# Choosing PSUM banks inside the list scheduler, loading the first conditioning weights by whole rows, holding back later quarters of x, and tracking small vectors by 8 bytes

## The chip, the cores and the metric

The kernel runs on the 8 cores of one Trainium2 chip. Each core computes one element of the batch, with no exchange between the cores; all of them read the same weights from HBM. The time of a run is the device time of the slowest core, in microseconds (us).

## What is computed

Two layers, each a mixing sub-layer and a channel sub-layer, over x of 2048 tokens by 1024 features. Float32 in and out; the kernel holds x as float32 and feeds TensorE with bf16.

```
mod = silu(c) @ w_ada + b_ada;  sh1, sc1, gt1, sh2, sc2, gt2 = split(mod, 6)
h = rms_norm(x, g_mix) * (1 + sc1) + sh1
q_a, k_a, v_a, q_b, k_b, v_b, gate_a, gate_b = split(h @ w_in)
q, k = rope(rms_norm(per head))                      # both mixers
y_a = banded attention (window 128, 8 heads, sinks) @ w_o_swa
y_b = block-sparse attention (own block + top 3 past blocks of 256) @ w_o_moba
x = x + gt1 * ((sigmoid(gate_a) * y_a + sigmoid(gate_b) * y_b) @ w_out)
h = rms_norm(x, g_mlp) * (1 + sc2) + sh2
x = x + gt2 * (square(relu(h @ w_up)) @ w_down)
```

## The kernel before

A Python program records every instruction of both layers with its operands (`Sched.add`), puts them in order with a list scheduler (`Sched.schedule`), and then emits one queue for each engine with semaphore waits (`emit`). Each engine works off its queue strictly in that order. Dependencies come from keys: an operand covers keys of 256 bytes in SBUF and of one 2048-byte bank in PSUM, and for each key the last writer and the readers are known. `window` gives each recorded operation a due time `vt`; among the operations that could start on an engine, the scheduler takes the one with the lowest `vt`. Its own costs of instructions and DMAs (L550 to L604) only decide the order.

The work of a layer, in the order in which it is recorded, over four quarters s of 512 tokens, each in a 16 KB slot of SBUF (`xslot`):

- **kv_stage(s)**: `norm_in_place` (squares on ScalarE at L776 or GpSimd at L779, a sum over features by 8 matmuls into one bank, Ln and Exp, then 8 pairs of scalar_tensor_tensor on VectorE, L577, and Identity at L791 that write h over half of the slot), then five `qk_item` (8 matmuls, Square, one matmul, Ln, Exp, a product, one matmul, three rotary products, using three banks) and four `v_block` (two banks each): 24 bank uses in a stage.
- **q_stage(s)**: eight `qk_item`. Those of quarters 2 and 3 run beside attention and use banks 6 and 7 only.
- **att_stage(s)** on banks 0 to 5, beside **c_mix** and **c_out** of the quarter before on banks 6 and 7; c_mix(3), c_out(2) and c_out(3) follow on all eight.
- **norm(s)** for the channel sub-layer, then `mlp_up` and `mlp_down` in four groups g over the four quarters, all eight banks.

A bank is chosen when the operation is recorded: `bank()` (L612) hands out the allowed banks in rotation. So a tile waits for all users of the tile that had its bank eight `bank()` calls earlier in the recorded order, whatever the scheduler makes of the order.

At the start SP issues the loads of x (`load_x`, 16 of 512 KB; 16 float32 128x128 transposes through PSUM for each two), the position rows and the spill of each x slot to HBM; GpSimd issues the weights. `ada_group(l, g, buffer)` loads 256 columns of w_ada (8 runs of 1 KB for each partition, written as 512 B of bf16) and makes two columns of `mod` from 16 one-column matmuls. Of layer 0, groups 0 to 7 (shift and scale of the mixing norm) come first, through five buffers; groups 8 to 23 are recorded behind the kv stages, four to each, and are first used by c_out and `norm`. `mod`, the gains and `A1` of a layer lie in one 256-byte stretch, and each group writes into it while each norm and each qk_item reads it. `rope_table` makes four tables, kept in HBM (`cs_d`), in two SBUF buffers `csb`. `load_w1` loads the five parts of w_in for q, k and v.

`norm` and `norm_in_place` share one buffer `nrm_r` and two `nrm_t` at T0, which is also where attention's probabilities and the operand `mixs[1]` of c_out(3) lie.

## Time and profile before

| | us |
|---|---|
| median of 3 runs | 2548.09 (2540.18 to 2724.18) |
| the profiled execution, device time | 2552.81 |
| its span on the slowest core (core 3) | 2551.3 |
| TensorE busy in it | 2179.7 (85%) |
| VectorE, ScalarE, GpSimd busy | 1138.2, 1126.0, 162.6 |
| spans of the eight cores | 2527.4 to 2551.3 |

Busy times are of the profiler's own modelled ends for matmuls, so a busy TensorE is not TensorE at its peak; the granted clock says at which of its levels (1.2 or 2.4 GHz) it ran. "Idle before, released by" on a row is the time in which the engine did nothing just before, and what ended it. Layer 0 runs from 0 to about 1343 us, layer 1 from there to the end.

### The profile page before, as it was taken

To read this page: it belongs to the slowest core of one execution; us is meant where nothing else is said; L and a number is where in the kernel's file an instruction comes from. 1 tells how busy PE (TensorE), PEld (TensorE's weight loads), DVE (VectorE), ACT (ScalarE), POOL (GpSimd) and SP (SyncE) were. 2 spreads that over 40 slices of the span, in tenths; PEclk is the share of its full clock that TensorE was granted. 3 is DMA by queue.
4 is the path that set the end of the run, shared out by engine and by line. 5 is a ranking of instruction groups with operands and counts; after the bars stand their busy time and mean duration, and the time that the engine had idled before them with its cause. 6 is when DMAs were issued, how large, how long until landed. Compare 5 with 4: busy or idle time off the path is not lost.

```text
span 2551.3 us, 33260 instructions; the slowest of 8 cores (2527.4 to 2551.3 us)
## 1 busy us (share of the span) xinstructions
PE 2179.7 (85%) x11604; PEld 905.6 (35%) x11604; DVE 1138.2 (45%) x1991; ACT 1126.0 (44%) x1650; POOL 162.6 (6%) x167
## 2 busy tenths in 40 slices
PE   1346687889899999999996687889899989999996
PEld 1323232323233444444442332232323434444443
DVE  1255576533322464444445677542422364444432
ACT  1444467666665341111115567857575452111122
POOL 1010120000000001010000020000000100000000
PEclk7677789999999999999997889999999999999998
DMA  9973420600002937373511020240000560331011
GB/s 212 195 134 42 63 46 7 94 34 1 34 1 50 156 51 95 41 106 42 100 67 58 17 50 9 37 64 34 1 34 1 107 92 14 53 51 16 1 67 66
DMA packets 122497, 149.28 MB, mean 59 GB/s; under 512 B 3808, under 2 KB 110560, under 8 KB 119264
## 3 DMA queue, kind: packets, MB, share of 16 engines
q0 software_dynamic: 108368, 85.14, 25.1%
q1 hardware_dynamic: 13968, 62.02, 7.1%
q8 instruction: 98, 1.61, 0.3%
q14 instruction: 63, 0.52, 0.1%
HBM read 205.02 MB, written 27.26 MB: 91 GB/s over the span
## 4 chain that ended last, share of the span: by engine, by line
PE 76%; ACT 8%; issue 5%; DVE 5%; DMA 4%; another core or an unknown queue 1%; POOL 0%; SPq 0%; ACTq 0%; DVEq 0%; POOLq 0%
PE PS L520 76%; ACT SB L546 4%; DMA SB<-w_ada 4%; DVE SB L577 2%; DVE SB L551 2%; ACT SB L791 1%; ACT SB L758 1%; PE PS L528 1%; ACT L546 1%; DMA SB<-w_in 1%; ACT SB L585 1%; DVE SB L567 0%; DVE SB L591 0%; ACT SB L776 0%
## 5 line engine op out<-in xcount | busy, mean ns | idle before, releaser
L520 PE MATMUL PS<-SB 128*128 128x512 bf16 (+7 forms) x11332 | 2138.9, 362 | 333.0 <-ACT SB L791 91.7
L520 PEld LDWEIGHTS PS<-SB 128*128 128x128 bf16 (+2 forms) x11332 | 866.3, 100 | 1598.9 <-issue 827.0
L546 ACT ACTIVATE SB<-PS 128x512 f32<-128x512 f32 (+4 forms) x902 | 642.8, 732 | 1032.6 <-PE PS L520 1010.2
L577 DVE SCALAR_TENSOR_TENSOR SB<-PS,SB 128x512 bf16<-128x512 f32 (+1 forms) x680 | 492.2, 728 | 669.4 <-ACT SB L546 348.6
L551 DVE TENSOR_TENSOR SB<-SB 128x512 bf16<-128x512 f32 (+5 forms) x452 | 254.6, 575 | 170.5 <-ACT SB L546 151.2
L551 DVE TENSOR_TENSOR SB<-PS,SB 128x512 f32<-128x512 f32 (+2 forms) x248 | 143.6, 585 | 172.5 <-PE PS L520 115.4
L577 DVE SCALAR_TENSOR_TENSOR SB<-SB,PS 128x512 f32<-128x512 f32 x128 | 87.6, 687 | 224.0 <-PE PS L520 148.0
L546 ACT ACTIVATE SB<-SB 128x512 f32<-128x512 f32 x226 | 139.9, 626 | 19.0 <-DVE SB L551 9.9
L577 DVE SCALAR_TENSOR_TENSOR SB<-SB 128x512 f32<-128x512 f32 x148 | 103.8, 726 | 38.6 <-ACT SB L546 25.9
L546 ACT ACT_TABLE_LOAD x67 | 86.0, 1283 | 40.1 <-DVE SB L551 21.2
L546 ACT ACTIVATE SB<-PS,SB 128x512 f32<-128x512 f32 x120 | 82.4, 687 | 47.4 <-PE PS L520 46.8
L585 ACT COPY SB<-PS 128x512 f32<-128x512 f32 x59 | 34.0, 586 | 141.6 <-PE PS L528 126.9
L604 POOL DMA_DIRECT2D SB<-w_ada x48 | 42.4, 885 | 449.6 <-PE PS L520 446.5
L791 ACT ACTIVATE SB<-SB 128x512 bf16<-128x512 f32 x64 | 45.0, 721 | 48.9 <-DVE SB L577 35.3
L528 PE MATMUL PS<-SB 128*128 128x128 f32 (+1 forms) x272 | 47.2, 327 | 20.9 <-DMA SB<-x 15.7
L746 POOL TENSOR_TENSOR SB<-SB 128x512 bf16<-128x512 f32 x20 | 20.8, 1038 | 622.4 <-PE PS L520 622.4
L528 PEld LDWEIGHTS PS<-SB 128*128 128x128 f32 (+1 forms) x272 | 39.6, 170 | 29.0 <-issue 24.9
L758 ACT ACTIVATE SB<-SB 128x512 bf16<-128x512 f32 x62 | 42.9, 719 | 13.1 <-DVE SB L577 13.0
L743 ACT ACTIVATE SB<-SB 128x512 bf16<-128x512 f32 x44 | 27.6, 627 | 43.8 <-DVE SB L577 43.7
L551 POOL TENSOR_TENSOR SB<-SB 128x512 bf16<-128x512 f32 (+1 forms) x26 | 37.2, 1431 | 134.5 <-DVE SB L551 90.7
L776 ACT ACTIVATE SB<-SB 128x512 bf16<-128x512 f32 x58 | 34.7, 624 | 15.4 <-PE PS L520 13.1
L587 DVE CAST SB<-PS 128x128 bf16<-128x128 f32 (+1 forms) x17 | 8.2, 480 | 59.8 <-PE PS L520 59.8
(22 smaller groups left out, 162.8 us busy)
## 6 DMA issues: line engine op xcount, KB each, us to landing
SB<-w_ada POOLq DMA_DIRECT2D x48, 512.0 KB, 8.4
SB<-w_in POOLq DMA_DIRECT2D x16, 1024.0 KB, 14.6
xsp<-SB SPq DMA_DIRECT2D x8, 2048.0 KB, 9.9
SB<-xsp SPq DMA_DIRECT2D x16, 1024.0 KB, 7.3
SB<-w_up POOLq DMA_DIRECT2D x16, 1024.0 KB, 13.0
SB<-w_down POOLq DMA_DIRECT2D x16, 1024.0 KB, 20.2
SB<-x SPq DMA_DIRECT2D x16, 512.0 KB, 15.7
SB<-cs SPq DMA_DIRECT2D x16, 512.0 KB, 4.4
```

Of the source, the lines that this page charges most:

```text
L520: ins = e.matmul(o, l_, rr, start=a, stop=b)
L528: S.add([('pe', lambda e, o=out.ap, i=in_.ap, d=ident.ap: e.transpose(o, i, d), 0.235 if in_.dt == F32 else 0.1)], list(in_.keys) + list(i ...
L546: S.add([('act', lambda e, o=out.ap, i=in_.ap: e.activation(out=o, in_=i, func=func, **kw), d)], r, out.keys, tab=TABS.get(func))
L551: return e.tensor_tensor(out=o, in0=a, in1=b, op=op)
L577: S.add([('dve', lambda e, o=out.ap, x=in0.ap, y=in1.ap: e.scalar_tensor_tensor(out=o, in0=x, scalar=a, in1=y, op0=op0, op1=op1), cost('dv ...
L585: alts.append((g, lambda e, o=out.ap, i=in_.ap: e.copy(out=o, in_=i), cost(g, n)))
L604: S.add([(eng, lambda e, o=out.ap, i=in_.ap: e.dma_start(out=o, in_=i), 0.45 if eng == 'sp' else 1.0)], in_.keys, out.keys, dma_key=key, n ...
L743: return e.activation(out=o, in_=i, func=AF.Square)
L746: return e.tensor_tensor(out=o, in0=i, in1=i, op=ALU.mult)
L758: return e.activation(out=o, in_=i, func=AF.Identity, bias=b)
L776: return e.activation(out=o, in_=i, func=AF.Square)
L791: return e.activation(out=o, in_=i, func=AF.Identity, bias=b)
```

## The change

It has five parts.

1. **Banks.** `bank()` goes away. A PSUM tile (`Tile`) is recorded without a bank and gets one in `schedule`, at the moment when its first operation is put in order: of the allowed banks the one that is free first by the scheduler's account (`place`). Tiles of one `line` get banks in their recorded order, and a tile with `more=True` gets one only if at least two of its allowed banks have no tile with operations still to be put in order. Allowed banks stay as they were.
2. **Tracking.** Operands between TR and TR+6144 (constants, `mod`, gains, routing vectors) have keys of 8 bytes instead of 256.
3. **First conditioning weights.** Groups 0 to 7 of layer 0 become eight loads of 128 rows by 2048 columns into eight buffers, 128 one-column matmuls that add up row block by row block in one bank, and one addition.
4. **x held back.** Quarter 1 of x is issued only when the sixth of these loads has landed, quarter 2 after the keys' weights (kb), quarter 3 after the values' (vb). Tables 2 and 3 of `rope_table` get buffers of their own in the last x slot, so 0 and 1 stay in `csb` and are not loaded again in the first two kv stages.
5. **Norm buffers.** `norm_in_place` rotates three `nrm_r` and four square buffers (one and two before). `norm` gets a scale row and one temporary of its own, apart from attention's buffers, and its 8 sum matmuls are recorded behind all 8 squares.

The scheduler also accounts for two DMA queues that share the bandwidth instead of one.

```diff
+        def place(tile):
+            if tile.line is not None and tile.line[tile.line[0]] is not tile:
+                return None, 1e9
+            if tile.more and sum(bank_free[b] < 1e8 for p in tile.allow for b in p) < 2:
+                return None, 1e9
+            best = None
+            for p in tile.allow:
+                f = max(bank_free[b] for b in p)
+                if best is None or f < best[1]:
+                    best = (p, f)
+            return best
...
+            for tl in op['tiles']:
+                if tl.banks is None:
+                    tl.banks = place(tl)[0]
+                    if tl.line is not None:
+                        tl.line[0] += 1
+                    for b in tl.banks:
+                        op['deps'].update(bank_users[b])
...
         def sb(off, shape, dt):
-            return SBA.view(off, shape, dt)
+            return (SBV if TR <= off < TR + 6144 else SBA).view(off, shape, dt)
...
-        nrm_r = sb(T0, (512,), F32)
+        nm_r, nm_t = sb(T0 + 30464, (512,), F32), sb(T0 + 32512, (512,), F32)
+        nrm_rs = [sb(T0 + o, (512,), F32) for o in (0, 8192, 10240)]
...
-        for g in range(8):
-            ada_group(0, g, (adab + adab2)[g % 5])
+        first = [sb(RW + 32768 + i * 4096, (2048,), BF16) for i in range(6)] + [
+            sb(T0 + 12288, (2048,), BF16), sb(T0 + 18176, (2048,), BF16)]
+        for k in range(8):
+            dma(first[k], Raw(w_ada_d[0, k * 128:(k + 1) * 128, 0:2048]), 'pool')
+        pm0 = ps((16,))
+        for k in range(8):
+            for j in range(16):
+                mm(pm0[:, j:j + 1], first[k][:, j * 128:(j + 1) * 128], silc[:, k:k + 1], k == 0 and j == 0, k == 7 and j == 15)
+        tt(modv(0)[:, 0:16], pm0, sb(VB + 16 * 4, (16,), F32), ALU.add)
         ada_fin(0, 0)
         W1 = load_w1(0, -70.0)
+        gates = [first[5].keys, W1['kb'].keys, W1['vb'].keys]
         for t in range(4, NT):
             at(-60.0 + t)
-            load_x(t)
+            load_x(t, gates[t // 4 - 1])
...
         def qk_item(wcols, s, gain, dest, cs):
-            pin = ps(bank(), (512,))
+            pin = ps((512,), more=True, line='qk')
```

GpSimd's queue at the start of the program. Before: five conditioning loads (128x8x256), then four of w_in, then the rest of the conditioning loads.

```order
L604 DMA SB<-cb 128x768
L604 DMA SB<-w_ada 128x8x256 x5
L604 DMA SB<-w_in 128x8x256
L604 DMA SB<-w_in 128x8x512 x3
L604 DMA SB<-w_ada 128x8x256 x6
L604 DMA SB<-w_in 128x8x512
```

Now:

```order
L696 DMA SB<-cb 128x768
L696 DMA SB<-w_ada 128x2048 x8
L696 DMA SB<-w_in 128x8x256
L696 DMA SB<-w_in 128x8x512 x3
L696 DMA SB<-w_ada 128x8x256 x3
L696 DMA SB<-w_in 128x8x512
L878 TENSOR_TENSOR SB<-SB 128x512 x2
```

All of the first conditioning weights now stand ahead of w_in; before, three of eight stood behind four loads of w_in.

ScalarE's queue where layer 0 passes from one kv stage to the next (before, from stage 1 to 2). L776 are the squares of the next quarter's norm, L791 its Identities that write h; L546 with SB<-PS,SB is an Ln, with SB<-SB an Exp, and L585 copies values out of PSUM.

```order
L546 ACTIVATE SB<-PS 128x512
L776 ACTIVATE SB<-SB 128x512 x2
L546 ACTIVATE SB<-PS,SB 128x512
L776 ACTIVATE SB<-SB 128x512
L546 ACTIVATE SB<-SB 128x512
L776 ACTIVATE SB<-SB 128x512 x3
L546 ACTIVATE SB<-PS,SB 128x512
L776 ACTIVATE SB<-SB 128x512
L546 ACTIVATE SB<-SB 128x512
L791 ACTIVATE SB<-SB 128x512 x8
L546 ACTIVATE SB<-PS 128x512
```

Now, inside a kv stage of layer 0 (L890 is the Identity, L638 the activations of the qk items, L677 the copies of values):

```order
L890 ACTIVATE SB<-SB 128x512
L638 ACTIVATE SB<-PS 128x512
L677 CAST SB<-PS 128x128
L890 ACTIVATE SB<-SB 128x512
L638 ACTIVATE SB<-PS,SB 128x512
L677 CAST SB<-PS 128x512
L638 ACTIVATE SB<-SB 128x512
L890 ACTIVATE SB<-SB 128x512
L638 ACTIVATE SB<-PS 128x512
L677 CAST SB<-PS 128x128
L890 ACTIVATE SB<-SB 128x512
```

The eight Identities no longer stand in one block between the last item of a stage and the first of the next; they are spread between the items and the value copies of the stage before.

## Rows read from the trace of the kernel before

**Rows 1.** The page: span, busy times, the span in 40 slices.
```profile
PE 2179.7 (85%) x11604; PEld 905.6 (35%) x11604; DVE 1138.2 (45%) x1991; ACT 1126.0 (44%) x1650; POOL 162.6 (6%) x167
PE   1346687889899999999996687889899989999996
PEclk7677789999999999999997889999999999999998
```

**Rows 2.** Busy time by stretch: stretch, its us, then each engine's busy us, clock, DMA, GB/s.
```profile
0.00:130.00 130.00, 34.44 (x264) 28.29 (x264) 28.79 (x61) 37.46 (x59) 14.05 (x20) 0.66 1.04 203
130.00:305.00 175.00, 102.89 (x669) 49.34 (x670) 92.28 (x186) 80.16 (x135) 16.07 (x17) 0.77 0.49 77
305.00:880.00 575.00, 512.84 (x2800) 179.05 (x2797) 256.89 (x490) 347.13 (x469) 43.45 (x41) 0.97 0.25 45
1343.00:1496.00 153.00, 98.60 (x483) 44.65 (x482) 90.20 (x168) 87.15 (x148) 3.11 (x3) 0.79 0.09 31
880.00:1343.00 463.00, 458.26 (x2460) 211.22 (x2459) 209.97 (x319) 105.45 (x173) 32.58 (x36) 1.00 0.48 74
```

**Rows 3.** Timeline of the start: start us, us, engine, line, what, idle before and releaser.
```profile
2.29 4.41 POOL L604 DMA_DIRECT2D SB<-w_ada  x5
6.64 3.56 POOL L604 DMA_DIRECT2D SB<-w_in  x4
28.35 0.88 POOL L604 DMA_DIRECT2D SB<-w_ada  x1 [18.15 <-PE PS L520]
97.64 0.56 PE L520 MATMUL PS<-SB 128*128 128x1 bf16 x16 [27.49 <-DMA SB<-w_ada]
106.65 0.17 DVE L577 SCALAR_TENSOR_TENSOR SB<-SB 128x8 f32<-128x8 f32 x1
```

**Rows 4.** DMA queues from 30 to 64 us: packets, MB, share of 16 engines' time.
```profile
q0 software_dynamic: 4848, 2.75, 67.7%
q1 hardware_dynamic: 866, 4.63, 42.7%
```

**Rows 5.** The page's DMA queues, whole span: packets, MB, share of 16 engines.
```profile
q0 software_dynamic: 108368, 85.14, 25.1%
```

**Rows 6.** Waits of TensorE, 130 to 350 us: total us, times, longest.
```profile
PE PS L520 <- ACT SB L791: 43.9, 4, 11.5
PE PS L520 <- DMA SB<-w_ada: 20.7, 4, 8.0
PE PS L520 <- DVE SB L551: 13.9, 2, 7.4
```

**Rows 7.** Waits of TensorE, 1280 to 1500 us.
```profile
PE PS L520 <- ACT SB L791: 47.7, 4, 13.0
```

**Rows 8.** Timeline of GpSimd: loads of c weights, released by the last kv matmuls.
```profile
305.59 0.88 POOL L604 DMA_DIRECT2D SB<-w_in  x1 [28.93 <-PE PS L520]
1496.09 0.94 POOL L604 DMA_DIRECT2D SB<-w_in  x1 [35.36 <-PE PS L520]
```

**Rows 9.** Timeline of TensorE where layer 1 begins.
```profile
1324.67 19.16 PE L520 MATMUL PS<-SB 128*128 128x512 bf16 x88
...
1357.35 21.68 PE L520 MATMUL PS<-SB 128*128 128x512 bf16 x114 [9.48 <-ACT SB L791]
```

**Rows 10.** Timeline of TensorE where layer 0's channel sub-layer begins.
```profile
879.15 17.64 PE L520 MATMUL PS<-SB 128*128 128x512 bf16 x81 [1.77 <-DVE SB L577]
```

**Rows 11.** Groups of instructions by shape: busy us, mean ns, idle before.
```profile
L528 PE MATMUL PS<-SB 128*128 128x128 f32 x256 | 43.7, 333 | 19.1 <-DMA SB<-x 15.7 <-ACT SB L585 1.7 <-DVE SB L551 1.5
L577 DVE SCALAR_TENSOR_TENSOR SB<-SB 128x512 f32<-128x512 f32 x144 | 103.2, 742 | 38.1 <-ACT SB L546 25.9 <-ACT SB L791 4.2 <-ACT SB L758 3.9
L791 ACT ACTIVATE SB<-SB 128x512 bf16<-128x512 f32 x64 | 45.0, 721 | 48.9 <-DVE SB L577 35.3 <-DVE SB L567 13.6
L551 DVE TENSOR_TENSOR SB<-SB 128x512 bf16<-128x512 f32 x153 | 107.1, 700 | 10.9 <-DVE SB L551 0.5 <-DVE SB L577 0.5 <-DVE SB L568 0.4
```

**Rows 12.** The page's DMA issues: count, KB each, median us from issue to landing.
```profile
SB<-w_ada POOLq DMA_DIRECT2D x48, 512.0 KB, 8.4
```

224 lines of the change are left out of this document (143 added, 81 removed).

## Prediction, made before the changed kernel ran

> **What bounds the kernel now.** I read the page first, for the share of TensorE by slice, then the busy times by stretch, then TensorE's waits in the stretches where it is not busy, and last the timeline at the places where those waits end. TensorE is busy 2179.7 of 2551.3 us and the two other large engines 44 to 45% each, so TensorE bounds the whole; but the 40 slices show that it does so unevenly: digits of 1 to 6 in the first five slices, a dip to 6 and 6 where layer 1 begins, 8 and 9 elsewhere [rows 1]. By stretch [rows 2]: 0 to 130 us TensorE is busy 34.4 of 130 with the DMA engines full (share 1.04); 130 to 305 (the four kv stages of layer 0) 102.9 of 175 at a granted clock of 0.77; the same stages of layer 1, 1343 to 1496, 98.6 of 153 at 0.79; attention and the c stages, 305 to 880, 512.8 of 575; the channel sub-layer 458.3 of 463. The last two have little to give. What can move lies in the first 305 us and in the 153 of layer 1.
>
> The first 106.7 us are a wait for conditioning weights. Five of the eight loads are issued at 2.3 us, then four loads of w_in; the sixth is issued at 28.4 us, when a buffer comes free, and its matmuls run at 97.6, after 27.5 us of idle TensorE. A1, which every h needs, is there at 106.65 [rows 3]. The kv stages end at about 305.6 and 1496.1, when the last matmul that reads their weights lets GpSimd load the next ones [rows 8]. Inside them TensorE waits 43.9 and 47.7 us, four times each, for the Identities of the in-place norm [rows 6, 7]: the norm of the next quarter does not overlap the matmuls of this one.
>
> **Part by part: the start.** At present the DMA engines are full, so this is a sum of engine time. From 30 to 64 us queue 0 moves 4848 packets, 2.75 MB, in 67.7% of 34 us of 16 engines: 76 ns for a packet of 0.57 KB. Queue 1, with x, takes 42.7% for 866 packets of 5.3 KB: 268 ns [rows 4]. The first eight groups are 8192 packets of 512 B, 39 us of all 16 engines. Now they are 1024 packets that read 8 KB and write 4 KB. No such packet is in the trace. Bounds: by the 5.3 KB packet, 268 ns, it is 17 us; by reading 8 KB at that packet's 20 GB/s, 400 ns, it is 26 us; at the small packets' rate per byte it stays 39. I take 25, since the float32 side is what has to be read. Ahead of A1 there are then also x's first quarter (2 MB, 6.5 us at 20 GB/s on 16 engines), a spill of 2 MB (6.5) and 4 to 5 for position rows and tables. With a start at 2.3 us: 45 us for A1 instead of 106.7.
>
> The Trainium skill (DMA: Bandwidth & Descriptors, Specifications) puts line rate at transfers of 512 B and more, which would leave nothing to gain from whole rows, since the old packets have that size on the writing side. The rows of queue 0 do not bear it out, at 7.5 GB/s written for one engine against 17 to 20 for the large packets of queue 1. By the rule A1 would stand at 59 us if the old 39 us are kept, 14 later.
>
> Then h(0) costs 8 pairs of 742 and 721 ns [rows 11] on two engines that overlap, 7 us: 52. The weights follow at the mean packet of queue 0, 0.251 x 2551 x 16 / 108368 = 94.5 ns [rows 5], 1024 packets and 6 us for each of kva, kb, vb. With x's quarter 1, held until the sixth load has landed, and a part of 2 between them, vb lands at about 25 + 18 + 31 (queue 1 so far: two and a half quarters of x, a spill, positions, tables) + 2 = 76 us. So stage 0 is fed through, about half of it after 76.
>
> **The kv stages of layer 0.** Matmul columns that TensorE has to do in 130 to 305: 102.9 us at clock 0.77. A stage holds 90 matmuls of 512 columns and 32 narrow ones; at the end of the channel sub-layer, at full clock, 88 matmuls of 512 take 19.16 us [rows 9], 0.218 each, so 19.6, about 2 for the narrow ones and 2 for its conditioning groups: 23.5 us, 94 for four. To that come 192 float32 transposes of quarters 1 to 3, which now fall behind 50 us instead of before 118; at 333 ns, mostly at the low clock [rows 11], 64, and at half of that 32; I take 36, the clock being mostly high. VectorE has 92.3 us in this stretch and ScalarE 80.2 [rows 2], plus 12 copies each, of about the length of a product: both near or under 100, so TensorE is longest with 130. Because banks are taken when work is put in order, and not eight calls back in the recorded order, and because the norm has its own rotating buffers, the squares and Identities of quarter s+1 stand between the items of quarter s (the two pieces of ScalarE's queue). Finer keys take away the order between each conditioning group's addition and each norm and gain, which stand behind the 20.7 and 13.9 us of waits for w_ada and L551 [rows 6]. I expect most of 43.9 + 20.7 + 13.9 = 78.5 us to go, and 20 to 25 to stay or come back: clock lows (130 us at 0.92 instead of 1.0 is 11) and waits for w_ada, which TensorE still takes in the order of its queue. 52 + 130 + 11 + 13 = 206, against 305.6: **minus 100**. The 16 groups behind need 16 x 1024 x 76 ns / 16 = 78 us of DMA between about 90 and 200, beside spills of 6 MB (20 us): it fits, with little to spare.
>
> **The kv stages of layer 1.** The norm of quarter 0 now takes place under the last mlp_down; before, it stood open from 1343.8 to 1357.4 [rows 9]. Its squares still cannot start before the last mlp_up has read the buffers they share. Four stages hold 4 x 21.5 = 86 us of TensorE at full clock; VectorE's 90.2 [rows 2] lose some 10 to GpSimd, which takes more of the 700 ns products [rows 11] (57 of them in its new queue, 26 in the old, half of the difference in each layer). Three engines near 80 to 90 us each, now overlapped: at 80% packing 110. In the new queue one norm, the last, still has its eight Identities in one block (7 us); that is within the 110. 153 - 110 = **minus 43**.
>
> **The rest.** The channel norm no longer waits for attention's buffers and c_out(3); TensorE idles there 1.8 us [rows 10], and I allow 1.2 for the gaps behind it: minus 3 for each layer, **minus 6**. Its single temporary makes a norm 8 x 1.7 = 13.6 us long, under 28 us of mlp matmuls for each quarter: nothing; without that cover 7 us once for each layer. Attention has the same order of exponentials and items in both queues (the sixteen last q items stand behind 0 to 59 exponentials in both), and the same banks: 0, with 10 either way. Two cs loads fewer: hidden.
>
> Sum: 2552.8 - 100 - 43 - 6 = 2404. The profiled execution lies 5 above the median; I say **2405** for the median, the 4 not being worth a digit.
>
> **The rivals.**
> - *Conditioning loads take over as the bound.* Each group's 16 matmuls stand at a fixed place in TensorE's queue, the three buffers are refilled only behind them, and GpSimd's squares and products stand behind waiting loads. From issue to landing one takes 8.4 us [rows 12], of which 78 / 16 = 5 are engine time; if the rest costs TensorE 2 us for each of the 16 groups, that is 32 us; the kv stages end near 238. For it: 20.7 us of such waits today at a slower pace. Against it: three are in flight at a time. 2437.
> - *The packing is better.* If the clock stays at 1.0 in both layers' stages and the waits go to nothing, 24 us go in layer 0 and 15 in layer 1: 2365. Against it: the clock was 0.77 and 0.79 with 59 to 64% busy.
> - *The norm chain stays on the path.* If ScalarE's and GpSimd's in-order queues only move the wait from Identities to something else (positions, rotary tables in front of GpSimd's squares, spills before h may be written), the kv stages keep 46 us each and only the start is won: 2552.8 - 60 - 6 = 2487. Against it: the order.
> - *Slower: starving on two banks.* With banks 6 and 7 alone, `more` wants both without open tiles, so a new item's or gate's 8 matmuls may be put in order only when the product that reads the last bank is. There are 64 such tiles in a layer (16 items, 48 gates). If each adds one reader, 0.75 us and the way there and back, 1.7 us, and attention's matmuls do not fill it, it is 64 x 2 x 1.7 = 218 us: 2620. It decides from 1.2 us a tile on. Against it: TensorE is 89% busy there with attention's own matmuls [rows 2], and its neighbours in the queue are as before.
>
> **Chances.** Forecast 0.60 (its own range 2380 to 2425), conditioning loads 0.16, better packing 0.12, norm chain 0.08, starving 0.04. A measurement of this kernel can tell about 2% from no change, so 2497 is the border. The first three are faster; of the norm chain, at 2487, six in ten; so 0.93 faster, 0.05 within 2%, 0.02 slower. The range takes in better packing and conditioning loads with 25 us more: 2360 to 2460.
>
> **What would show it.** A1's addition in the timeline at 40 to 60 us, all eight loads landed before any of w_in; the loads of c weights behind the kv stages issued near 205 instead of 305.6, and 110 us instead of 153 behind the end of layer 0's channel sub-layer; TensorE's waits for the Identity line under 15 us in each layer; a clock of 0.85 or more in both stretches; 575 us from the end of the kv stages to the channel sub-layer, as now. Wrong would be: A1 later than 70 (packets of 8 KB no better than small ones), waits of TensorE for w_ada above 30 us, VectorE or ScalarE over 90% busy in the kv stages, or more than 590 us for attention.

## The result, and the profile after

The changed kernel takes 2435.26 us (median of 4 runs, 2432.23 to 2547.38) against 2544.14 for the kernel before beside it (2539.87 to 2724.18). The ratio is 0.957, with a 95% interval of 0.954 to 0.960: faster by 109 us. The forecast was 2405 (a sum of 149 us less, counted from the profiled execution of the kernel before). The time lies inside the range on record and 30 us above the forecast. In the longest executions of both kernels the cores of one die ran at a lower granted clock; ratios and profiles leave such executions out.

The page of the profile after, core 6 (busy time and share; then busy tenths in 40 slices, the granted clock in tenths of full speed, and the DMA engines' busy tenths):

```profile
span 2430.7 us, 32875 instructions; the slowest of 8 cores (2414.1 to 2430.7 us)
PE 2144.9 (88%) x11383; PEld 903.5 (37%) x11604; DVE 1128.1 (46%) x1950; ACT 1105.1 (45%) x1631; POOL 235.1 (10%) x222
...
PE   1469878897999999999998777889899999999997
...
PEclk9879889999999999999999898999999999999998
DMA  9966405100105837474320201600010542240012
```

Against [rows 1] the start has shrunk: TensorE is at 7 to 9 from the fourth slice on (before, from the sixth), and the dip where layer 1 begins has gone from 6 to 7. The page lacks 221 of TensorE's matmul records (11383 against 11604 weight loads), and its busy time with them. The six cores that have all records show 2166.5 to 2171.0 us, against 2172.5 to 2179.7 on the six such cores of the kernel before. So the work is nearly the same, some 7 us less, and almost the whole gain is idle time.

Busy times by stretch, the same five stretches as [rows 2], at this kernel's own borders (kv stages of layer 0 end at 232, the first w_up load is at 760, layer 0 ends at 1269, the kv stages of layer 1 at 1383):

```profile
core 6: us, PE busy (x) PEld busy (x) DVE busy (x) ACT busy (x) POOL busy (x), PEclk, DMA share, GB/s
0.00:130.00 130.00, 44.77 (x321) 30.20 (x326) 40.88 (x78) 43.35 (x67) 14.20 (x23) 0.90 1.00 210
130.00:232.00 102.00, 82.28 (x561) 41.98 (x572) 76.11 (x151) 63.76 (x117) 36.30 (x31) 0.90 0.55 94
232.00:760.00 528.00, 461.12 (x2552) 157.86 (x2599) 237.40 (x463) 339.26 (x457) 47.29 (x43) 0.95 0.21 38
1269.00:1383.00 114.00, 88.73 (x468) 41.38 (x478) 87.00 (x156) 74.04 (x132) 37.27 (x27) 0.90 0.11 41
760.00:1269.00 509.00, 505.63 (x2643) 234.80 (x2696) 226.68 (x341) 115.87 (x189) 38.68 (x45) 1.00 0.53 83
```

In the kv stages TensorE is now busy 78 to 81% of the time (some records of this core are missing, so slightly more) at a clock of 0.90, where it was 59 to 64% at 0.77 and 0.79 [rows 2].

A marker in each trace cuts the span into six parts: GpSimd's first load of c weights (the end of the kv stages, the answer to [rows 8]), its first w_up load, and SP's last spill of the layer.

```profile
232.08 0.87 POOL L696 DMA_DIRECT2D SB<-w_in  x1
759.94 0.89 POOL L696 DMA_DIRECT2D SB<-w_up  x1 [12.88 <-PE PS L612]
1268.86 0.32 SPq L696 DMA_DIRECT2D xsp<-SB  x1
1383.02 0.96 POOL L696 DMA_DIRECT2D SB<-w_in  x1 [30.29 <-PE PS L612]
1901.21 0.96 POOL L696 DMA_DIRECT2D SB<-w_up  x1 [19.96 <-PE PS L612]
```

| us | start and kv stages, layer 0 | attention | channel | kv stages, layer 1 | attention | channel | span |
|---|---|---|---|---|---|---|---|
| before | 305.6 | 520.6 | 518.1 | 151.8 | 509.1 | 546.1 | 2551.3 |
| after | 232.1 | 527.9 | 508.9 | 114.2 | 518.2 | 529.5 | 2430.7 |
| difference | -73.5 | +7.3 | -9.2 | -37.6 | +9.1 | -16.6 | -120.6 |
| on record | -100 | 0 | -3 | -43 | 0 | -3 | -149 |

TensorE's waits in layer 0 from 130 to 233 us, and in layer 1 from 1260 to 1384 (releaser: us in total, times, longest), which answer [rows 6] and [rows 7]:

```profile
PE PS L612 <- ACT SB L890: 12.2, 2, 9.4
PE PS L612 <- ACT SB L875: 2.0, 4, 0.6
PE PS L612 <- DVE SB L669: 1.8, 4, 0.9
...
PE PS L612 <- ACT SB L890: 13.6, 1, 13.6
PE PS L612 <- ACT SB L875: 7.1, 6, 4.9
PE PS L612 <- DVE SB L669: 2.6, 3, 1.1
```

L890 is the Identity of the in-place norm. TensorE waited for it 43.9 and 47.7 us, four times a layer. In layer 0 the norm of quarter 0 now falls before 130 us, so the whole stretch from 0 to 233 us has to be counted; there it is

```profile
PE PS L612 <- ACT SB L890: 16.0, 3, 9.4
```

that is 3.7 us for the norm of quarter 0, 9.4 for quarter 1, nothing for quarter 2 and 2.8 for quarter 3. In layer 1 the one wait stands before the last quarter: three stages run through and the fourth waits for its whole norm.

```profile
1363.73 20.57 PE L612 MATMUL PS<-SB 128*128 128x512 bf16 x110 [13.57 <-ACT SB L890]
```

### The profile page after: what moved, and what is told of

It is laid out like the page before. It is cut to its first block, busy times and chain, and to the rows that moved or that the text cites. A ratio compares the mean times of both kernels' runs of the same rounds, so it can differ in the third digit from the quotient of the medians.

```text
span 2430.7 us, 32875 instructions; the slowest of 8 cores (2414.1 to 2430.7 us)
## 1 busy us (share of the span) xinstructions
PE 2144.9 (88%) x11383; PEld 903.5 (37%) x11604; DVE 1128.1 (46%) x1950; ACT 1105.1 (45%) x1631; POOL 235.1 (10%) x222
## 4 chain that ended last, share of the span: by engine, by line
PE 81%; ACT 6%; issue 5%; DVE 5%; DMA 2%; another core or an unknown queue 0%; POOL 0%; SPq 0%; ACTq 0%; DVEq 0%; POOLq 0%
PE PS L612 79%; ACT SB L638 4%; DVE SB L643 2%; DMA SB<-pos 2%; DVE SB L669 2%; PE PS L620 1%; ACT L638 1%; ACT SB L677 0%; ACT SB L890 0%; DVE SB L659 0%; POOL SB L893 0%; DVE SB L683 0%; DMA out<-SB 0%; SPq L696 0%
## 5 line engine op out<-in xcount | busy, mean ns | idle before, releaser
L612 PE MATMUL PS<-SB 128*128 128x512 bf16 (+6 forms) x11111 | 2115.1, 362 | 231.0 <-ACT SB L638 78.8
L612 PEld LDWEIGHTS PS<-SB 128*128 128x128 bf16 (+2 forms) x11332 | 864.9, 100 | 1454.9 <-issue 679.6
L638 ACT ACTIVATE SB<-PS 128x512 f32<-128x512 f32 (+4 forms) x902 | 641.6, 732 | 973.2 <-PE PS L612 953.7
L669 DVE SCALAR_TENSOR_TENSOR SB<-PS,SB 128x512 bf16<-128x512 f32 (+1 forms) x680 | 493.9, 727 | 665.8 <-ACT SB L638 343.1
L643 DVE TENSOR_TENSOR SB<-SB 128x512 bf16<-128x512 f32 (+5 forms) x421 | 234.0, 567 | 146.3 <-ACT SB L638 132.5
L643 DVE TENSOR_TENSOR SB<-PS,SB 128x512 f32<-128x512 f32 (+3 forms) x241 | 141.7, 596 | 132.7 <-ACT SB L638 75.3
L669 DVE SCALAR_TENSOR_TENSOR SB<-SB,PS 128x512 f32<-128x512 f32 x128 | 87.5, 686 | 214.0 <-PE PS L612 138.4
L638 ACT ACTIVATE SB<-SB 128x512 f32<-128x512 f32 (+1 forms) x226 | 139.6, 624 | 27.3 <-DVE SB L659 11.6
L669 DVE SCALAR_TENSOR_TENSOR SB<-SB 128x512 f32<-128x512 f32 (+1 forms) x148 | 118.4, 810 | 32.5 <-ACT SB L638 16.1
L643 POOL TENSOR_TENSOR SB<-SB 128x512 bf16<-128x512 f32 (+1 forms) x57 | 76.9, 1356 | 348.0 <-DVE SB L669 299.8
L638 ACT ACTIVATE SB<-PS,SB 128x512 f32<-128x512 f32 x120 | 81.8, 685 | 36.5 <-PE PS L612 34.7
L620 PE MATMUL PS<-SB 128*128 128x128 f32 (+1 forms) x272 | 56.6, 314 | 37.6 <-DMA SB<-x 28.6
L677 ACT COPY SB<-PS 128x512 f32<-128x512 f32 x59 | 34.0, 583 | 117.7 <-PE PS L620 90.1
L620 PEld LDWEIGHTS PS<-SB 128*128 128x128 f32 (+1 forms) x272 | 39.3, 162 | 55.0 <-issue 43.0
L858 ACT ACTIVATE SB<-SB 128x512 bf16<-128x512 f32 x60 | 43.2, 720 | 23.6 <-DVE SB L669 22.7
L890 ACT ACTIVATE SB<-SB 128x512 bf16<-128x512 f32 x51 | 36.3, 720 | 26.4 <-DVE SB L669 23.9
L696 POOL DMA_DIRECT2D SB<-w_up x16 | 14.1, 881 | 281.5 <-PE PS L612 281.5
L875 ACT ACTIVATE SB<-SB 128x512 bf16<-128x512 f32 x47 | 27.2, 621 | 27.8 <-PE PS L612 26.8
L842 ACT ACTIVATE SB<-SB 128x512 bf16<-128x512 f32 x46 | 28.8, 627 | 21.8 <-DVE SB L669 21.8
```

The costliest lines, as they stand in the source:

```text
L612: ins = e.matmul(o.ap, l_.ap, rr.ap, start=a, stop=b)
L620: S.add([('pe', lambda e, o=out, i=in_, d=ident: e.transpose(o.ap, i.ap, d.ap), 0.235 if in_.dt == F32 else 0.1)], list(in_.keys) + list(i ...
L638: S.add([('act', lambda e, o=out, i=in_: e.activation(out=o.ap, in_=i.ap, func=func, **kw), d)], r, out.keys, tab=TABS.get(func))
L643: return e.tensor_tensor(out=o.ap, in0=a.ap, in1=b.ap, op=op)
L669: S.add([('dve', lambda e, o=out, x=in0, y=in1: e.scalar_tensor_tensor(out=o.ap, in0=x.ap, scalar=a, in1=y.ap, op0=op0, op1=op1), cost('dv ...
L677: alts.append((g, lambda e, o=out, i=in_: e.copy(out=o.ap, in_=i.ap), cost(g, n)))
```

## Experiments: which part does it

Each kernel below is the changed kernel with the edit shown, or where it is said the kernel with split keys; its spans are cut by the same markers, on its slowest core unless others are named. Intervals of a ratio are 95%. A time without a ratio is that of the profiled execution.

**Banks taken in rotation again**, in the recorded order of each bank; the rules `line` and `more` go with it, all else is kept:

```diff
+            if tile.fix is not None:
+                for b in tile.fix:
+                    if tile.bankq[b][tile.bankq[b][0]] is not tile:
+                        return None, 1e9
+                return tile.fix, max(bank_free[b] for b in tile.fix)
...
+            if allow is None:
+                t.fix = nxt('bank', pool_banks[0])
```

> The changed kernel with one part undone: PSUM banks are again handed out in rotation when a tile is recorded (tiles of one bank strictly in recorded order, no rule of two free banks). Keys of 8 bytes, whole-row conditioning loads, held x and the norm buffers stay. Theory A, the choice of banks while ordering is what lets the in-place norm run under the stage before: the holes of about 9 us before each stage come back in both layers, the kv stages take about 145 us in layer 1 instead of 115, and the time is 2495 to 2515 us. Theory B, the norm's own rotating buffers and the finer keys are enough: under 2450 us and still about 115 us in layer 1.

Measured: ratio 1.011 (1.009 to 1.014), 2563.95 us, in the theory's direction and further than it said. The kv stages of layer 0 end at 283.6 and those of layer 1 last 149.3; the channel sub-layers take 528.4 and 557.6 us. TensorE's waits in the kv stages of layer 1:

```profile
PE PS L636 <- ACT SB L914: 50.1, 4, 13.7
```

L914 is the Identity here: four waits of 12 us, as before [rows 7]. Without the choice of banks the four other parts together leave the kernel slower than it was, so that choice carries the layer 1 gain, most of layer 0's (51.5 of 73.5 us), and it is what makes the rest fit. The choice of banks with the four other parts undone was not run, so what it is worth alone is not shown.

**Only the start** (whole-row weights, x held back and the tables' own buffers; rotation, 256-byte keys and the old norm buffers):

> Only the start is changed: whole-row conditioning loads into eight buffers, x held back, tables 2 and 3 in buffers of their own. Banks in rotation, keys of 256 bytes, one scale row and two square buffers for the in-place norm, the channel norm sharing attention's buffers. Theory A, the start is worth what A1 gained, 38 us (106.7 to 68.5), and the rest of the 109 comes from the kv stages: 2495 to 2510 us, with 150 us again in layer 1's stages. Theory B, the start carries most, since DMA-bound work moves with it: under 2465 us.

Measured: ratio 0.995 (0.993 to 0.997), 2526.75 us, above both ranges. The kv stages of layer 0 end at 290.1, 15.5 us earlier than before, and those of layer 1 last 151.0. A1 is there at 65.4 us and not at 106.7 [rows 3], and yet only 15 of these 41 us reach the end of the kv stages. The start alone is worth about 0.5%. This kernel is faster than the rotation kernel, which has the finer keys and the new norm buffers besides: under rotation these two cost more than they bring.

**x not held back**:

```diff
-            load_x(t, gates[t // 4 - 1])
+            load_x(t)
```

> The changed kernel with quarters 1 to 3 of x no longer held back, all else kept. Theory A, x's large packets crowd out the weights: A1 moves from 68.5 to 80 us or later, and the time is 2445 to 2460 us. Theory B, the DMA engines are full to 160 us with the same bytes whatever the order, and A1 waits for the rotary tables, not for the loads: 2428 to 2442 us, the values' weights landing within 5 us of 97 and the kv stages of layer 0 ending within 6 us of 232.

Measured: 2444.5 us in the profiled execution, 12 more than with the hold; kv stages end at 251.8. The time borders on theory A's, but A1 does not come later: it is there at 64.5 us, 4 earlier than with the hold. TensorE's waits from 0 to 252 us:

```profile
PE PS L612 <- DMA SB<-w_ada: 41.1, 2, 30.0
PE PS L612 <- ACT SB L890: 35.9, 3, 15.0
```

The hold is worth 20 us in the kv stages of layer 0, of which 12 are taken back in the attention stretch behind them (515.6 instead of 527.9): without it the transfers of x push a conditioning load from its place and TensorE stands 30.0 us before it.

**Keys of 256 bytes everywhere**:

```diff
-        SBV = Arena('SBV', sbt, 8)
+        SBV = Arena('SBV', sbt, 256)
```

> The changed kernel with keys of 256 bytes for the small vectors again, all else kept. Theory A, the additions of the conditioning groups and the norms and gains are put in a fixed order again, and a norm waits for four loads of w_ada: layer 0's kv stages 15 to 30 us longer, layer 1 unchanged, 2450 to 2465 us. Theory B, the norms wait for the same loads anyway through the engines' queues and the full DMA engines: 2430 to 2440 us.

Measured: ratio 0.959 (0.957 to 0.962), the same as the changed kernel within the intervals, but not by the same road. The kv stages of layer 0 end at 266.8, 35 us later, with waits for w_ada back (17.4 us in four); and the two attention stretches take 513.3 and 500.1 us, 14.6 and 18.1 less. So the finer keys win 35 us in one place and lose 33 in two others, and the prediction, which counted only the first, had taken attention as unchanged. The time fell into theory B's range, whose ground (the norms wait for the same loads anyway) did not hold; theory A had the ground and half of the size.

## Experiments: where the finer keys lose

The keys cover two sets of vectors: constants, `mod`, gains and `A1`; and, behind them, what routing uses (block means, their padded form, gate scores, ranks, biases). One run for each:

```diff
-            return (SBV if TR <= off < TR + 6144 else SBA).view(off, shape, dt)
+            return (SBV if TR <= off < TR + 4608 else SBA).view(off, shape, dt)
```

The second run has `TR + 4608 <= off < TR + 6144` instead. In both, three small views are taken through `sb` too, so that readers and writers have the same keys.

> Keys of 8 bytes only for the constants, mod, gains and A1; the routing vectors (block means, their padded form, gate scores, biases, ranks) get keys of 256 bytes again. Theory: the 35 us that fine keys win in the kv stages of layer 0 come from mod and A1, and the 15 and 18 us that they cost in the two attention stretches come from the routing vectors. Then the kv stages end near 232, the stretch from there to the first w_up load takes 513 us in layer 0 and 500 in layer 1, and the time is 2400 to 2405 us. Rival: the 15 and 18 us are no property of either set of keys but of which order the scheduler happens to find: 518 to 530 us in one layer or both, 2420 to 2440 us.

> The complement: keys of 8 bytes only for the routing vectors, 256 bytes for the constants, mod, gains and A1. Theory: kv stages of layer 0 end near 267 us as with 256 bytes everywhere, attention stretches of 528 and 518 us as in the changed kernel, 2465 us. Rival (order found by chance): the kv stages near 267, attention anywhere between 500 and 530, 2433 to 2465 us.

Measured with 8 bytes for the first set only: 2394.1 us in the profiled execution, 2403.4 in a second one. The kv stages end at 230.4, attention takes 504.2 and 504.2, and layer 1's kv stages 114.7. With 8 bytes for routing only: ratio 0.963 (0.960 to 0.966), kv stages at 266.6, attention 509.1 and 520.5. The win belongs to the first set in both runs. The loss follows the second set in layer 1 (518 and 521 with fine routing keys, 500 and 504 without) and less cleanly in layer 0 (528 and 509 with, 513 and 504 without): there part of it is the order that the scheduler happens on. Among all kernels that choose banks while ordering, the two attention stretches sum to 1008 to 1016 us in the five with split keys and 1013 in the one with 256 bytes everywhere, and to 1030 to 1046 in the five with fine routing keys. In layer 1 no core of the first six takes more than 507.5 us and none of the others less than 512.7; in layer 0 the two sets of cores overlap. (With rotation it is 1043 with fine keys, 1018 in the kernel with only the start changed and 1030 in the kernel before.) TensorE's waits in the attention stretch of layer 0, in the changed kernel and then with split keys:

```profile
PE PS L612 <- ACT SB L638: 38.3, 38, 2.8
PE PS L612 <- DVE SB L643: 21.4, 27, 2.1
PE PS L612 <- issue: 4.5, 22, 0.5
```

```profile
PE PS L612 <- ACT SB L638: 27.6, 38, 2.6
PE PS L612 <- DVE SB L643: 18.8, 29, 1.8
```

The same waits: these two lines went from 59.7 to 46.4 us. Which instruction of the routing is ordered worse with fine keys was not isolated. Taking them back wins 38 us of the span in the profiled executions (2392.5 against 2430.7), and 1.5 percentage points in the ratios of the two kernels below that add an edit to the split keys (0.942 against 0.957).

## Experiments: what holds the start

The last addition before A1 stands at 68.2 us, not at 45. The rows of VectorE ahead of it in the changed kernel, with that addition, then those of ScalarE and of TensorE, where L875 are the squares of the first norm and L659/L669 the arithmetic of the rotary tables:

```profile
56.18 0.43 DVE L679 CAST SB<-SB 128x512 f32<-128x512 int32 x1 [6.80 <-DMA SB<-pos]
...
68.24 0.17 DVE L643 TENSOR_TENSOR SB<-PS,SB 128x16 f32<-128x16 f32 x1 [1.89 <-PE PS L612]
```

```profile
58.74 0.63 ACT L638 ACTIVATE SB<-SB 128x512 f32<-128x512 f32 x1 [11.64 <-DVE SB L659]
60.07 0.63 ACT L638 ACTIVATE SB<-SB 128x512 f32<-128x512 f32 x1 [0.70 <-DVE SB L669]
60.60 1.13 ACT L875 ACTIVATE SB<-SB 128x512 bf16<-128x512 f32 x2
```

```profile
61.88 1.44 PE L612 MATMUL PS<-SB 128*128 128x512 bf16 x3 [16.11 <-ACT SB L875]
```

The eight loads had all landed by 45 us (the last of their packets starts at 42.9). The last 16 conditioning matmuls stand in TensorE's queue behind the norm's sum, that behind squares in ScalarE's queue, those behind the Sin of table 2, and that behind a position row whose load was issued only when the row before had been used. Two kernels move A1 in opposite directions. First, position rows in four buffers:

```diff
-            posi, x = sb(P0, (512,), I32), sb(P0 + 2048, (512,), F32)
+            posi, x = sb(RW + 16384 + s * 2048, (512,), I32), sb(P0 + 2048, (512,), F32)
```

> The four position rows get four buffers, so that their loads are issued together instead of one behind each table; nothing else changes. Theory: in the changed kernel A1's addition at 68 us was held by the rotary tables (ScalarE's Sin of table 2 at 59, the squares of the first norm behind it, the last 16 conditioning matmuls behind the norm's sum), not by its weights, which had landed by 45. Then A1 comes at 48 to 54, and quarter 1 of x is issued near 45 instead of 61. How much of these 15 us reaches the end: theory says 10, the kv stages of layer 0 end near 222, 2425 us. Rival: the DMA engines are full until 160 us in either case, so A1 comes early but the values' weights still land near 97 and the kv stages end at 229 to 234: 2433 to 2437 us.

Measured: ratio 0.951 (0.947 to 0.955), 2426.4 us in the profiled execution. The addition is at 64.6 instead of 68.2, the kv stages end at 232.8, the attention of layer 0 takes 514.9. The theory's 48 to 54 was wrong; the rival's end was right, and the time is below the rival's because attention is shorter. Second, the first weights by columns again, into the eight buffers:

```diff
-        for k in range(8):
-            dma(first[k], Raw(w_ada_d[0, k * 128:(k + 1) * 128, 0:2048]), 'pool')
...
+        for g in range(8):
+            ada_group(0, g, sb(first[g].off, (8, 256), BF16))
```

> One part undone: layer 0's first conditioning weights come again as eight loads of 256 columns (8192 packets that write 512 bytes), but into the eight separate buffers, all ahead of w_in; everything else as in the changed kernel. Theory (the price on record: small packets cost 76 ns of an engine each, 39 us of all 16; whole rows showed 268 to 337 ns for 1024 packets, about 19): the eighth load lands near 65 us instead of 45, and because the DMA engines stay full until about 160 us everything behind it is 20 us later as well: the values' weights at 115 instead of 97, the kv stages of layer 0 end near 248 instead of 232, 2450 us. Rival (a written 512 bytes is already at full rate): the eighth load again near 45 and 2435 us.

Measured: ratio 0.953 (0.950 to 0.957), not slower. The last addition is at 76.6, 8 us later, and the kv stages end at 229.8, 2 us earlier. Queue 0 (packets, MB, share of 16 engines) in the column kernel from 0 to 62 us, then in the changed kernel from 0 to 45; both have moved the same 4.56 MB by then:

```profile
q0 software_dynamic: 8653, 4.56, 64.8%
```

```profile
q0 software_dynamic: 1632, 4.56, 66.4%
```

0.648 x 62 is 40 us of all engines, 0.664 x 45 is 30: whole rows save 10 us, not the 20 that this run was built to show. The expectation had divided a window's time by all its packets, of which a part are small. By size, the 1024 packets that write 4096 bytes took 409 ns each in the changed kernel (26 us of all engines), and those that write 512 bytes 72 ns in the column kernel (37 us for 8192). So about 10 us of DMA time and 8 us of A1 are really saved, and none of it reaches the end.

> Split keys (2394 us) together with the four position rows in buffers of their own. Alone, the position rows brought A1 from 68 to 65 us, not to 50, the end of the kv stages stayed at 232.8, and the attention stretch of layer 0 was 13 us shorter (515 instead of 528). Theory: that gain was of the same kind as the split keys' (another order found for the routing), so it doesn't add: 2390 to 2397 us. Rival: the two are independent and add: 2382 us.

Measured: ratio 0.942 (0.940 to 0.945), 2402.2 us in the profiled execution, 5 above the theory's range: with split keys the position rows add nothing, as the theory said; their gain alone was in attention.

## Experiments: why the kv stages end at 230 to 233

In the changed kernel and in six edits of it (column loads, position rows, split keys, the last two together, and the two that follow, which stand on the split keys) the kv stages of layer 0 ended between 229.8 and 233.1 on the slowest core, wherever A1 stood. TensorE's rows between 109 and 131 us show what stands there (12 groups of four float32 transposes of x between 108.6 and 133 us, of which some are shown):

```profile
110.01 0.63 PE L620 MATMUL PS<-SB 128*128 128x128 f32 x4 [0.61 <-ACT SB L677]
...
114.57 1.09 PE L620 MATMUL PS<-SB 128*128 128x128 f32 x4 [0.93 <-ACT SB L677]
116.48 1.08 PE L620 MATMUL PS<-SB 128*128 128x128 f32 x4 [0.82 <-ACT SB L677]
```

Each group waits for ScalarE's copy of the one before, as it must if all of them go through one bank. (No row names the bank; with two banks kept for them, below, the order one by one is gone.) Two attempts took away what was suspected first. **Two banks kept for the transposes:**

```diff
+        XB = [(b,) for b in range(6, 8)]
...
-                pv = ps((4, 128))
+                pv = ps((4, 128), allow=XB if t >= 4 else None)
...
+                pool_banks[0] = [(b,) for b in range(6)] if l == 0 and s < 2 else ALL
                 kv_stage(l, s, W1)
```

> On top of the kernel with split keys (8 bytes for constants and mod, 256 for the routing vectors; 2394 us): the transposes of x's quarters 1 to 3 may use PSUM banks 6 and 7 only, and the items of the first two kv stages banks 0 to 5 only. In the changed kernel 12 groups of four transposes from 108 to 131 us follow one another through a single bank, each behind ScalarE's copy of the one before (1.5 to 2.0 us a group, TensorE idle 0.6 to 0.9 before each), since open tiles hold the others. Theory: this stands on the path to norm(1) and stage 1; with two banks a group costs its own 1.1 us, the row of groups ends about 10 us earlier, and so do the kv stages: end near 222 instead of 230, 2384 us. Rival: the DMA and the clock set the end of the kv stages, as two earlier runs hint, where an A1 of 65 or 77 us instead of 68 left the end at 230 to 233: again 229 to 233, 2392 us. Second rival: six banks are too few for the items: 240, 2402 us.

Measured: 2402.6 us in the profiled execution, kv stages end at 232.8. The transposes no longer go one by one, and in their place TensorE stands at a conditioning group:

```profile
125.17 2.72 PE L612 MATMUL PS<-SB 128*128 128x1 bf16 x21 [18.31 <-DMA SB<-w_ada]
```

**Conditioning groups 8 to 23 later:**

```diff
-                    S.window(i0, T + s * 17.0, T + s * 17.0 + 17.0)
+                    S.window(i0, T + 60.0 + s * 30.0, T + 90.0 + s * 30.0)
```

> On top of the split keys (2394 us): conditioning groups 8 to 23 of layer 0 get later due times (60 to 180 us on the scheduler's clock instead of 0 to 68), so that they stand among the q stages and attention instead of the kv stages. Theory (the rival of the prediction in which conditioning loads hold the kv stages): squares on GpSimd no longer stand behind loads that wait for TensorE, norm(1) is 9 us earlier, and 16 groups of one-column matmuls leave the kv stages; they end near 215, and attention takes 6 us more: 2383 us. Other view: the groups fill gaps of TensorE in the kv stages, where it is 75% busy, and stand in its way in attention, where it is 90% busy: kv end 224, attention 514, 2396 us.

Measured: ratio 0.942 (0.940 to 0.943), 2398.3 us, kv stages end at 233.1, attention 510.6. The time gains nothing. But here the slowest core misleads. The other seven cores of this kernel end their kv stages between 216.3 and 223.1:

```profile
216.29 0.94 POOL L696 DMA_DIRECT2D SB<-w_in  x1 [10.89 <-PE PS L612]
```

```profile
233.13 0.94 POOL L696 DMA_DIRECT2D SB<-w_in  x1 [10.89 <-PE PS L612]
```

(cores 7 and 2). The median core ends at 221.5, with split keys alone at 229.6, and attention in layer 0 takes back the 8 us (509.9 against 502.0 on the median core). That is close to the expectation's other view.

What tells the cores apart is in ScalarE's rows. In the changed kernel the first copy of a v tile (128x128) out of PSUM comes right behind the copies of x, although its matmuls were done by 109 us, and the next norm's squares stand behind the rest of the first stage:

```profile
130.22 0.58 ACT L677 COPY SB<-PS 128x512 f32<-128x512 f32 x1 [1.32 <-PE PS L620]
131.60 0.27 ACT L677 CAST SB<-PS 128x128 bf16<-128x128 f32 x1 [0.79 <-PE PS L620]
...
143.56 1.14 ACT L875 ACTIVATE SB<-SB 128x512 bf16<-128x512 f32 x2
```

The row of the v copy names its releaser: L620, TensorE's transposes of x, and not the L612 matmuls that made the tile. k and v are written into the 32 KB in which x is staged, eight buffers of 4 KB, used twice. So v of the first stage may be written only when quarter 3 of x has been transposed out of its buffers; quarter 3 is what the change holds back longest (issued at 97 us). Meanwhile finished v tiles keep their banks, and the transposes share what is left.

The same link holds on every core. First copy of v and end of the kv stages, lowest to highest of the eight cores, and how far the end lies behind the copy of the same core:

| us | first copy of v | kv stages end (median) | end behind the copy |
|---|---|---|---|
| changed kernel | 116.0 to 131.6 | 219.3 to 232.2 (229.1) | 100 to 105 |
| column loads | 124.4 to 133.5 | 222.6 to 230.9 (226.2) | 97 to 100 |
| position rows | 118.3 to 123.9 | 220.9 to 233.1 (227.5) | 103 to 105, two cores 110 and 111 |
| split keys | 115.1 to 128.5 | 217.1 to 230.6 (229.6) | 101 to 103 |
| split keys, position rows | 117.2 to 127.5 | 221.1 to 231.8 (228.9) | 103 to 106 |
| split keys, two banks for x | 121.1 to 134.9 | 219.0 to 232.8 (227.6) | 98 to 99 |
| split keys, groups later | 116.8 to 132.2 | 216.3 to 233.1 (221.5) | 99 to 101 |

In all 56 the v copy is released by L620. Moving the groups brought it forward by 6 us on the median core (121.7 against 127.3); whether by the groups' place or by the moment at which the weights that hold quarter 3 back landed was not separated.

**Quarter 3 staged where the q weights come later**, on top of the split keys:

```diff
-            xi = xin[t % 8]
+            xi = xin[t % 8] if t < 12 else sb(RW + 16384 + (t - 12) * 4096, (8, 128), F32)
...
+        at(-40.0)
+        load_w1q(0, W1)
```

> On top of the split keys (2394 us, kv stages of layer 0 end at 230.4): x's quarter 3 is staged in the 16 KB that the q weights take later, instead of in the last four of the eight staging buffers; the two q weight loads are recorded behind it. Nothing else changes. Theory: the end of the kv stages stood at 230 to 233 in every run, whatever was done to A1, banks or conditioning groups, because k and v of stage 0 are written over the staging buffers of x. Held back as it is, quarter 3 is issued at 97 us and transposed by about 131, and only then come the copies of stage 0's v (first at 131.6 in the changed kernel), whose open tiles leave one bank for the transposes meanwhile, and the norm of quarter 1 behind them at 143. With other buffers the copies come from about 105 on, the norm of quarter 1 near 120, h(1) near 140 instead of 161, and of these 20 us at least 12 reach the end: kv end 212 to 218, 2374 to 2382 us. Rival: the loads of the conditioning groups take over, which land up to 125 us and held TensorE for 18 us when two banks were kept for the transposes: kv end 228 to 233, 2392 us.

(`load_w1q` holds the loads of the q weights, now recorded behind those of x.) Measured: ratio 0.938 (0.935 to 0.941), and the kv stages end at 214.4. The first v copy comes at 101 us (127.9 with split keys alone), the norm of quarter 1 feeds TensorE at 145 instead of 161, and from 90 us on TensorE waits 0.9 us for w_ada. Quarter 3 is issued at the same time as with split keys alone (93.3 and 92.6 us), so it is where it is staged that counts, not when it comes:

```profile
101.47 0.26 ACT L677 CAST SB<-PS 128x128 bf16<-128x128 f32 x1
```

```profile
145.19 18.37 PE L612 MATMUL PS<-SB 128*128 128x512 bf16 x113 [7.94 <-ACT SB L896]
```

```profile
214.36 0.88 POOL L696 DMA_DIRECT2D SB<-w_in  x1 [4.48 <-PE PS L612]
```

On the slowest core no other edit had moved this end forward by more than 2.3 us; this one did by 16, inside what the theory named (212 to 218). On the median core it is 13.7 us (215.9 against 229.6), the eight cores lie between 212.4 and 220.2, and the end no longer hangs on the v copy, which is 112 to 120 us ahead of it. The time did not follow: the profiled execution took 2391.8 us, which is the rival's number and not the theory's 2374 to 2382; the others that the ratio takes lie between 2377.3 and 2393.6. Layer 1's first w_up load is still 13 us earlier than with split keys alone (1849.3 against 1862.4), but the span of the slowest core only 2 (2390.2 against 2392.5): its granted clock was 0.87 in its last 140 us, where the other kernel's was 0.95 and six of its own cores had 0.94. The ratio is the lowest of all that were run, 1.9 percentage points below the changed kernel's 0.957, but its interval touches those of the other kernels with split keys (0.942, 0.940 to 0.943 and 0.940 to 0.945). That the kv stages end earlier is clear of noise; how much of it the time keeps is not.

## Why the prediction was right, and where it was off

- **What bounds the kernel, and the main mechanism: right.** The start and the two sets of kv stages gave 111 of the 121 us of span. The waits for the Identity line went from 43.9 and 47.7 to 16.0 and 13.6 us (under 15 in each layer was on record: missed by 1 us in layer 0), the waits for w_ada behind 130 us to nothing. The rotation run shows the choice of banks to be the part that does it.
- **Layer 1's kv stages: -37.6 for -43.** 110 us were forecast at 80% packing, 114.2 came at 78%, and the 153 that they were taken from is 151.8 by the markers. The term that was too small is the norm of the last quarter: its eight Identities in one block were put at 7 us, and TensorE waited 13.6 for them. The first norm, forecast as hidden, cost 4.9 us for its squares. The clock was 0.90, as asked for.
- **A1 at 45: failed.** The sum of DMA time up to there was right: the loads had landed by 45, and the 1024 packets cost 26 us where 25 were taken from the bound by what is read (409 ns a packet, 400 on record). The step left out was the order of three queues between the last weight and the last matmul. It is off by 23 us. The rival "the norm chain stays" named rotary tables in front of squares, for the wrong place. The DMA sum behind A1 fell short: the values' weights were put at 76 us, and quarter 3, which waits for them, was issued at 97.
- **161 us from A1 to the end of the kv stages: right in number (163.9), by luck.** It was built as 7 us for h(0), TensorE's 130 and 24 of waits. Core 4, which ends at the same time and has nearly all records, was busy 117 us of the 164 and idle 47:

```profile
68.30:232.23 163.93, 116.69 (x729) 61.66 (x730) 95.73 (x184) 90.20 (x158) 40.06 (x35) 0.85 0.77 151
```

  Too much work and too few waits cancelled. And the last addition at 64.6, 68.2 and 76.6 gave the same end within 3 us, on the slowest core (232.8, 232.1, 229.8) as on the median one (227.5, 229.1, 226.2). What set it was a dependency that the prediction had not looked for: the hold on x delays its staging buffers, which k and v overwrite. The cost of the hold was reckoned as DMA order alone. With this freed the end is at 214.4, 8 us from the 206 on record.
- **x's transposes: miscounted.** The prediction put 192 of quarters 1 to 3 at 36 us. There are 96 (12 loads of eight), and they kept TensorE busy for 18.9 us; half of them, in 12 groups behind one another's copies, took 24 us of its queue.
- **Attention 0, with 10 either way: failed by 6.** It takes 7.3 and 9.1 us longer. The order of exponentials and items was compared and found alike; the order of the routing's small instructions, which finer keys free, was not. With split keys it is 504.2 in both layers, and 500 to 515 in the four kernels built on them.
- **The channel sub-layers: mis-sized to the other side.** 6 us were allowed for both layers, 25.8 came. Waits for the norm's products (6.4 us in layer 0; 6.6, and 5.0 for copies, in layer 1) are gone; the forecast had counted the one of 1.8 us [rows 10] and its neighbours only. In the rotation run, which has the norm's own buffers too, these stretches are longer than before (528.4 and 557.6), and with rotation and the old buffers they are as before (517.1 and 546.0). So the buffers alone do not bring it; whether the choice of banks does without them was not run.
- **The rivals.** Conditioning loads as the bound (2437) came nearest to the time, but not by its mechanism: on the profiled core TensorE does not wait for w_ada behind 130 us, moving the groups late changed the time by nothing (the end on the median core by 8 us, which attention took back), and waits for them of 11 to 18 us only came when the transposes were given two banks. Starving on two banks did not come: the attention stretch kept its matmul time.

The errors cancel in part: +26.5 in the first part, +5.4 in layer 1's kv stages, +16.4 in attention, -19.8 in the channel sub-layers, 28 us together.

## What to carry to other kernels

When an edit delays a transfer on purpose, list what else its buffer holds: here the weights came earlier, as wanted, and the results of the first stage waited for the delayed quarter, because they lie in its staging space. When one marker stays put under several unlike edits, stop adjusting what TensorE is seen waiting for and look for the instruction that became free last; what it waits for can be a write over a buffer, and then the row names as its releaser the last reader of the old contents. Look at all cores before calling a marker fixed: the slowest is the maximum of eight, and here the others ended up to 17 us earlier. And a finer dependency is not a gain everywhere: give it to the vectors on the path and measure the others by themselves.

## What the runs showed of the hardware

Packets on the DMA engines, from float32 in HBM to bf16 in SBUF: one that writes 512 bytes took 72 ns of an engine (7.1 GB/s written, column kernel, 0 to 62 us); one that writes 4 KB and reads 8 KB took 409 ns (10.0 GB/s written, changed kernel, 0 to 45 us), 0.7 as much per byte. The Trainium skill (DMA: Bandwidth & Descriptors, Specifications) gives 512 B as the least size for line rate; with a conversion on the way these rows do not agree. Nor did it matter for the time: the saved 10 us of engine time did not reach the end.

The granted clock in the kv stages came out otherwise than expected. From 100 to 130 and from 130 to 160 us, in the changed kernel and then with the new staging:

```profile
100.00:130.00 30.00, 19.21 (x105) 11.83 (x105) 7.04 (x10) 11.10 (x19) 2.03 (x2) 0.73 1.10 250
130.00:160.00 30.00, 19.11 (x123) 9.70 (x124) 17.64 (x39) 19.86 (x38) 11.94 (x11) 0.84 0.97 190
```

```profile
100.00:130.00 30.00, 26.88 (x204) 16.49 (x200) 21.70 (x40) 20.52 (x38) 10.12 (x11) 1.00 1.09 277
130.00:160.00 30.00, 19.08 (x100) 8.37 (x101) 18.61 (x35) 15.29 (x25) 6.10 (x7) 0.72 0.80 152
```

The mean clock was 1.00 in the stretch in which TensorE was busy 26.9 of 30 us, and 0.73 and 0.84, for a part of the time at 1.2 GHz, where it was busy 19 and went through the transposes in groups of four with gaps. With the new staging the low stretch is still there, one step later, around the gap in front of the norm of quarter 1. Work without gaps does not always bring the full clock: with position rows in buffers of their own the norm of quarter 1 came to TensorE at 157 instead of 165 us, the clock was 0.56 from 100 to 130 us, and from 160 to 190 us it was 0.79 on a core that was hardly idle:

```profile
160.00:190.00 30.00, 29.48 (x154) 13.96 (x153) 22.15 (x33) 17.15 (x29) 5.62 (x4) 0.79 0.00 1
```

Two cores of that kernel show it (0.70 and 0.72 from 100 to 230 us, against 0.82 to 0.84 on the six others), and they are the two whose kv stages end at 233, 4 to 12 us behind the others. So there a part of what the earlier start gave was taken back by the clock. What kept it low on these two is not shown.
